# Expert product of a decoder step: every second chunk in plain fp32, and another order of stores, word gathers and row gathers

## What is computed

```python
qry = (hc @ w_query).reshape(-1, PEER_HEADS, 2, PEER_HALF)
...
top_s, pos = lax.top_k(cand_s, PEER_TOPK)
idx = jnp.take_along_axis(cand_i, pos, axis=-1)
gate = jax.nn.softmax(top_s, axis=-1).astype(hc.dtype)
act = jax.nn.gelu(jnp.einsum('cd,chkd->chk', hc, expert_u[idx]))
return jnp.einsum('chk,chkd->cd', gate * act, expert_v[idx])
```

## Time and profile before

| | us |
|---|---|
| median of 3 runs | 2215.64 (2212.16 to 2217.15) |
| the profiled execution's own time | 2217.63 |
| its span, first to last instruction | 2215.9 |
| DVE busy / ACT busy / POOL busy | 1620.5 / 1120.8 / 785.4 |
| PE busy | 2166.3 |
| down stage, pass 0 | 1548.6 to 1896.7 |
| down stage, pass 1 | 1896.7 to about 2198 |

### The profile page before, as it was taken

How to read it: one execution, slowest core, us unless ns; L and a number is a source line. 1 busy time by engine, 2 the same in 40 slices (tenths; PEclk the granted TensorE clock), 3 DMA queues, 4 the chain that set the end, 5 groups by cost and what they waited for, 6 DMA issues and landing times.

```text
span 2215.9 us, 53111 instructions
## 1 busy us (share of the span) xinstructions
PE 2166.3 (98%) x16578; PEld 2128.9 (96%) x16578; DVE 1620.5 (73%) x2983; ACT 1120.8 (51%) x2094; POOL 785.4 (35%) x612
## 2 busy tenths in 40 slices
PE   9999999999999999999999999999889999999997
PEld 8999899999999999999999999999789999999997
DVE  8778688886766767888885444466567787788886
ACT  6445366667455445555555444455333444444453
POOL 0321100002011000888888888200577433222231
PEclk9999999999999999999999999999999999999998
DMA  7887656666556556877776878698899999899995
GB/s 245 292 292 248 224 185 199 207 210 209 182 187 204 176 173 182 192 179 190 189 185 179 204 185 188 179 314 260 273 320 307 350 390 379 313 369 371 369 365 191
DMA packets 303834, 546.01 MB, mean 246 GB/s; under 512 B 77072, under 2 KB 116456, under 8 KB 303600
## 3 DMA queue, kind: packets, MB, share of 16 engines
q1 hardware_dynamic: 227024, 427.68, 59.6%
q0 software_dynamic: 60064, 105.07, 16.0%
q10 hardware_dynamic: 16640, 12.06, 1.8%
HBM read 519.39 MB, written 25.28 MB: 246 GB/s over the span
## 4 chain that ended last, share of the span: by engine, by line
PE 65%; POOL 5%; issue 3%; DMA 2%; DVE 2%; ACT 0%; DVEq 0%; SPq 0%; ACTq 0%
PE ps L317 15%; PE ps L320 15%; PE ps L316 15%; PE ps L2207 8%; PE ps L2220 5%; PE ps L2211 5%; POOL gu L1790 3%; DMA gat<-expert_v,gidx 2%; POOL gat L1639 1%; DVE lo L1623 0%; PE ps L2251 0%; DMA raw<-weights 0%; PE ps L1403 0%; DMA gu<-u_spill,gidx 0%; DVE gacc L2085 0%
## 5 line engine op out<-in xcount | busy, mean ns | idle before, releaser
L304 DVE TENSOR_TENSOR lo<-raw,hi 128x512 fp32r<-128x512 f32 x995 | 685.8, 697 | 365.6 <-ACT hi L299 345.0
L299 ACT CAST hi<-raw 128x512 fp32r<-128x512 f32 x995 | 608.1, 620 | 471.9 <-PE ps L320 447.2
L316 PE MATMUL ps<-h_hi,hi 128*128 128x264 f32 (+1 forms) x3200 | 821.8, 286 | 1.0 <-DVE h_lo L957 1.0
L317 PE MATMUL ps<-h_lo,hi 128*128 128x264 f32 (+1 forms) x3200 | 820.1, 286 | 0.0
L316 PEld LDWEIGHTS ps<-h_hi,hi 128*128 128x128 f32 x3200 | 601.8, 188 | 7.9 <-issue 6.3
L317 PEld LDWEIGHTS ps<-h_lo,hi 128*128 128x128 f32 x3200 | 602.0, 188 | 0.3 <-issue 0.2
L1773 POOL DMA_INDIRECT w_spill<-chosen,widx x256 | 432.4, 1689 | 264.5 <-DVE widx L1998 186.8
L320 PE MATMUL ps<-h_hi,lo 128*128 128x264 f32 (+1 forms) x3200 | 523.3, 285 | 2.1 <-DVE lo L304 1.9
L320 PEld LDWEIGHTS ps<-h_hi,lo 128*128 128x128 f32 x3200 | 444.3, 188 | 3.8 <-DVE lo L304 3.6
L2207 PE MATMUL ps<-whl,hi 128*128 128x368 f32 x1544 | 348.7, 348 | 6.4 <-DVE whl L2077 5.2
L1639 POOL DMA_INDIRECT gat<-expert_v,gidx x160 | 178.0, 1112 | 315.4 <-DVE gacc L2085 297.4
(11 more groups left out here) (308 smaller groups left out, 2294.4 us busy)
## 6 DMA issues: line engine op xcount, KB each, us to landing
raw<-u_tiles SPq DMA_DIRECT2D x512, 256.0 KB
raw<-weights SPq DMA_DIRECT2D x480, 256.0 KB
raw_v<-expert_v SPq DMA_DIRECT2D x128, 512.0 KB
raw<-expert_v SPq DMA_DIRECT2D x124, 512.0 KB
w_spill<-zeros ACTq DMA_DIRECT2D x16, 736.0 KB, 5.6
wld<-w_spill SPq DMA_DIRECT2D x32, 368.0 KB, 4.1
u_spill<-ust SPq DMA_DIRECT2D x128, 40.0 KB
qb<-q_spill POOLq DMA_DIRECT2D x8, 512.0 KB, 5.9
```

What stands on the lines that cost most here:

```text
L299: nc.scalar.copy(hi[k % SPLIT][:], raw_quarter(k)).then_inc(hi_done, 1)
L304: nc.vector.tensor_tensor(lo[k % SPLIT][:], raw_quarter(k), hi[k % SPLIT][:].bitcast(F32), ALU.subtract).then_inc(lo_done, 1)
L316: pe.matmul(out, a, rhs[0][:, first + j, 0:n], start=start and j == 0, stop=False)
L317: pe.matmul(out, a, rhs[1][:, first + j, 0:n], start=False, stop=False)
```

## The change

Plain chunks are 1, 3, 5 and 7 of each turn (not chunk 1 of pass 0 and not the last): 126 of 256. SP stores the last tile of `u_spill` after one load of the stage instead of four. POOL starts rows after 5 words instead of 10; then it issues two words behind each of the first five rows, and from there one and two by turns. There are four row buffers instead of three (the fourth takes the place of a gate buffer that is no longer used). In pass 0 rows are added from step 3 of turn 1 on, four in that turn, five a turn in turns 2 to 7, six in turns 8 to 13. DVE stops for words before turns 1, 2, 4, 7 and 10 (before: 1, 3, 6 and 9). The residual comes back in four loads of 540,672 bytes, all before the loads of turn 4, instead of 16 loads of one sixteenth spread over the pass. The rest of the diff gives all engines one common semaphore for increments that nothing waits for.

```diff
-NATIVE = (3, 7)
+NATIVE = (1, 3, 5, 7)
...
+    gat3 = place("gat3", at["raw_v"] + 2 * 4 * 4 * TD, [P, HALF * P])
+    gacc = place("gacc", at["gat3"], [P, len(GROUPS), HALF * P])
...
-    gat.append(gat2)
+    gat += [gat2, gat3]
+    ROWS = len(gat)
...
-    BOUNDS = (1, 3, 6, 9)
+    BOUNDS = (1, 2, 4, 7, 10)
     FIVE, SIX = (1, 2, 3, 5, 6), (1, 2, 3, 5, 6, 7)
-    ADDS = [[()] + 7 * [FIVE] + 4 * [SIX] + [SIX, FIVE, FIVE, (0, 1, 2, 3, 4)], 15 * [FIVE] + [(0, 1, 2, 3, 4)]]
+    ADDS = [[(), (3, 5, 6, 7)] + 6 * [FIVE] + 6 * [SIX] + [FIVE, (0, 1, 2, 3, 4)], 15 * [FIVE] + [(0, 1, 2, 3, 4)]]
+    WORDS_AT = (0, 5, 15, 30, 50, TG)
...
-        for s in range(RAW, SLOTS):
+        load_expert(0, 0, RAW)
+        spill(PAIR_U - 1, 1)
+        for s in range(RAW + 1, SLOTS):
             load_expert(0, 0, s)
-        spill(PAIR_U - 1, 1)
...
-        sp.dma_start(x2[:, 0], x2_dram[:, 0]).then_inc(x2_in, 16)
-        sp.dma_start(x2[:, KD - 1], x2_dram[:, KD - 1]).then_inc(x2_in, 16)
...
+        x2_back(0)
+        with sp.Fori(1, CHUNKS - UP_CHUNKS - 1) as i:
+            for s in range(SLOTS):
+                load_expert(0, i + 1, s)
+                if s == 2:
+                    sp.wait_ge(w_mul, UP_CHUNKS + i + 4)
+                    cells_in(UP_CHUNKS + i + 1, 1)
+            x2_back(i)
+        x2_back(3)
...
-        for n in range(FIRST_WORDS):
+        words = WORDS_AT[1]
+        for n in range(words):
             gather_u(n)
...
+        for n in range(2 * TG):
+            if n == ROWS - 1:
+                pool.wait_ge(w_mul, UP_CHUNKS + 3)
+            if n >= ROWS:
+                pool.wait_ge(gat_used, n - ROWS + 2)
             gather_rows(n)
-            if n == TG + 2:
+            for _ in range(min(1 if n > ROWS and n % 2 else 2, TG - words)):
+                gather_u(words)
+                words += 1
+            if n == TG + ROWS - 1:
```

More of the change, by code:

```diff
@@ L1489, in mid_vector @@
                 dve.wait_ge(raw2_hi, t + 1)
-                dve.sem_inc(dve_go, 1)
+                dve.sem_inc(go, 1)
                 nc.vector.scalar_tensor_tensor(out=raw2[1][:, t, :], in0=x[:, t, 0:LIVE],
@@ L1548, in program @@
     sel_seen = sem("sel_seen")
-    gat_in, gat_used = [sem(f"gat_in{b}") for b in range(3)], sem("gat_used")
-    gu_in = [sem(f"gu_in{b}") for b in range(4)]
+    gat_in, gat_used = [sem(f"gat_in{b}") for b in range(4)], sem("gat_used")
+    gu_in = [sem(f"gu_in{b}") for b in range(5)]
     gw_made, gacc_zero = sem("gw_made"), sem("gacc_zero")
@@ L1578, in program @@
     G_FIRST = [sum(GROUPS[:g]) for g in range(len(GROUPS))]
-    WORD_TURNS = [-(-sum(len(a) for a in ADDS[0][:i]) // TURN) * TURN for i in BOUNDS] + [TG]
-    FIRST_WORDS = WORD_TURNS[1]
+    assert all(sum(len(a) for a in ADDS[0][:i]) <= n for i, n in zip(BOUNDS[1:], WORDS_AT[1:]))
     def column(n):
@@ L1735, in load_expert, with x2_back @@
             sp.dma_start(expert_slot(s).rearrange("p a b -> p (a b)"), expert_v[p, 8 * i + s]).then_inc(expert_in(s), 16)
-        for s in range(RAW, SLOTS):
+        def x2_back(q):
+            at_q = slice(4 * q, 4 * q + 4) if isinstance(q, int) else bass.ds(4 * q, 4)
+            sp.dma_start(x2[:, at_q], x2_dram[:, at_q]).then_inc(x2_in, 16)
+        load_expert(0, 0, RAW)
+        spill(PAIR_U - 1, 1)
+        for s in range(RAW + 1, SLOTS):
             load_expert(0, 0, s)
-        spill(PAIR_U - 1, 1)
         load_expert(0, 1, 0)
@@ L1744, in experts_sync @@
             load_expert(0, 1, s)
-        sp.dma_start(x2[:, 0], x2_dram[:, 0]).then_inc(x2_in, 16)
-        sp.dma_start(x2[:, KD - 1], x2_dram[:, KD - 1]).then_inc(x2_in, 16)
[L1747 to L1754, removed]
+        x2_back(0)
[7 more added lines that the diff above has]
+        x2_back(3)
+        with sp.Fori(CHUNKS - UP_CHUNKS - 1, NK // 8 - 1) as i:
+            for s in range(SLOTS):
+                load_expert(0, i + 1, s)
         with sp.Fori(0, NK // 8) as i:
@@ L1788, in gather_u @@
         def gather_u(n):
-            j, batch = column(n), max(b for b in range(4) if n >= WORD_TURNS[b])
+            j, batch = column(n), max(b for b in range(len(BOUNDS)) if n >= WORDS_AT[b])
             nc.gpsimd.indirect_dma_start(gu[:, j:j + 1], None, u_rows,
@@ L1792, in gather_u @@
                 .then_inc(gu_in[batch], 16)
-        for n in range(FIRST_WORDS):
+        words = WORDS_AT[1]
+        for n in range(words):
             gather_u(n)
[L1795 to L1798, removed]
-            gather_rows(n)
[L1800 to L1806, removed]
-            if n == TG + 2:
+        for n in range(2 * TG):
[3 more added lines that the diff above has]
+                pool.wait_ge(gat_used, n - ROWS + 2)
+            gather_rows(n)
+            for _ in range(min(1 if n > ROWS and n % 2 else 2, TG - words)):
+                gather_u(words)
+                words += 1
+            if n == TG + ROWS - 1:
                 pool.wait_ge(mm_done, 2 * C0 + 2 * NK + SPLIT)
@@ L2080, in add_rows @@
         def add_rows(n):
-            j, b = column(n), n % 3
+            j, b = column(n), n % ROWS
             g = 0 if j < GROUPS[0] else 1
-            dve.wait_ge(gat_in[b], 16 * (n // 3) + 16)
+            dve.wait_ge(gat_in[b], 16 * (n // ROWS) + 16)
             dve.wait_ge(gat_used, n + 1)
@@ L2088, in weigh_rows @@
         def weigh_rows(b):
-            first, last = WORD_TURNS[b] // TURN, WORD_TURNS[b + 1] // TURN
-            dve.wait_ge(gu_in[b], 16 * (WORD_TURNS[b + 1] - WORD_TURNS[b]))
+            first, last = WORDS_AT[b] // TURN, WORDS_AT[b + 1] // TURN
+            dve.wait_ge(gu_in[b], 16 * (WORDS_AT[b + 1] - WORDS_AT[b]))
             for rows_of in (slice(first, last), slice(GROUPS[0] + (TURN - 1) * first, GROUPS[0] + (TURN - 1) * last)):
@@ L2124, in after_pass @@
             if p == 0:
-                dve.wait_ge(x2_in, 16 * KD)
+                dve.wait_ge(x2_in, 16 * KD // 4)
             def hi_part(m):
```

17 lines of the change are left out of this document (8 added, 9 removed).

## The result

The changed kernel takes 2196.7 us (median of 4, 2194.77 to 2200.54); the kernel before, with one more run beside it, 2214.0 (2212.16 to 2217.15). The ratio is 0.9923, with a 95% interval of 0.9903 to 0.9942: 17 us faster, 0.8%. The forecast was 2195, in a range of 2184 to 2210. The profiled execution took 2195.4 us, span 2193.7.

The account below looks back on a forecast made before the run. POOL's gathers were taken to bound pass 0, with PE waiting through DVE, and PE to bound pass 1. Pass 0 -30 and pass 1 +8.6 gave net -21.5 on 2217.63, 2196; forecast median 2195, range 2184 to 2210 us.

Parts of the forecast that it names:

- The total: Whole kernel: net -21.5 us on the profiled 2217.63 gives 2196; 2195 us forecast for the median.
- Plain chunks on PE: PE, both passes: four chunks take 9.50 us instead of 9.23, 0.27 us for each chunk replaced.
- the count of passes: Skill's four array passes for true fp32: plain product a third dearer, 63 chunks about 47 us, no gain.
- Pass 1, +8.6 us: Pass 1, where PE is the path: 32 split chunks made plain lengthen it by 8.6 us, to about 310.
- PE's sum: PE's work in a pass before the change: 32 groups of four chunks, 295.4 us, and the fold, 3.6: 299.0 us.
- The store and the five words: Start of pass 0: POOL starts about 1553.5, 9.5 us earlier; DVE's 11.8 us stop and PE's 9.64 idle go.
- The stop before turn 10: Pass 0, DVE waiting for all 80 words: DVE stops about 5 us, PE about 2; 4 us for all stops.
- The DMA sum, 318 us: Pass 0's next limit: 285.4 us of bytes at 384 GB/s, 19 for words, 5.6 early idle, 8.3 at the end.
- The residual, 0 (at the other end 4 us): Pass 0, turns 1 to 3: 1.5 MB moved early costs nothing if later turns take it back, else 4 us.
- PE alone: Rival, chance 0.12: the DMAs keep up, pass 0 is 311 us or less, the time 2188 or below.
- New waits on top: Rival, chance 0.11: word stops, early residual and clock falls add; pass 0 328 to 335 us, time 2204 to 2211.
- No change: Rival, chance 0.08: DMAs hold only 332 to 341 GB/s; pass 0 335 to 344 us, time 2211 to 2220.

Follow-up runs that it names:

- half_orders: words_in_time with two plain chunks a turn (3 and 7) and pass 0's loads of expert_v cut to half a chunk from turn 1 on; 2174.0 us.
- plain_first_late: words_in_time with two plain chunks a turn in pass 1 (four in pass 0) and the residual in 16 loads over the pass; 2178.6 us.
- words_in_time: Changed kernel with the last batch of words cut in two: 65 due before turn 10, all 80 before turn 13; 2188.9 us.
- late_store: Changed kernel with the last store of the up products behind four loads again; 2198.5 us, ratio 0.9931 to the kernel before.
- half_loads: words_in_time with each load of expert_v in pass 0 from turn 1 on bringing only half the chunk; 2182.8 us.

## Why the prediction held, and where it did not

- *The total:* 2195 for 2196.7 is better than its parts, and that is luck. Pass 0 fell by 25.9 us instead of 30, pass 1 rose by 3.2 instead of 8.6, and the two errors cancel. (2196 less 2.0 for the median is 2194, not 2195; that changes nothing.)
- *Plain chunks on PE:* right. Four chunks take 9.50 us, pass 1 is 307.2 in six of the eight kernels with four plain chunks a turn in that pass, and the trace decided rightly against the count of passes.
- *Pass 1, +8.6 us:* too much for the two profiled executions, where it was +3.2. The sum took 301.3 us for pass 1 from a window that ended before the last products. To the start of the last sums it was 304.0, of which 5 us were above PE's sum, lost at the fold at the pass's end: DVE's last add came 0.52 us late, and the granted clock from 2194 to 2198 was 0.50. The changed kernel's execution does not lose them, but others do (last section), so part of the +3.2 is chance too. Between executions in which the clock stays up, pass 1 is 299.5 us with two plain chunks (half_orders, plain_first_late) and 307.2 with four: 7.7 us, not far from the 8.6 that the text charged.
- *The store and the five words:* right in every event (1553.13 for 1553.5, no stop before turn 1). But what they are worth was read from the idle PE that they take away, 9.64 us; the store, undone alone, costs 1.7 us of pass 0.
- *The stop before turn 10:* the step that failed. The text had DVE stop 5 us and PE 2, put 4 us down for all stops "and none on top of what follows". DVE stopped 8.16 us, PE idled 6.60, and with the half clock it made most of 8.8 us of pass 0 (322.2 against 313.4). The reckoning let row 48 wait for the add of row 44, some 4 us ahead of the stop. But that add ended at 1743.98, and row 48 only went out at 1746.41: POOL never waited for an add from 1712 to 1758, it was itself behind, and the last word went out 1.1 us after DVE was at the stop.

```profile
1742.70 1.28 DVE L2091 SCALAR_TENSOR_TENSOR gacc<-gat,gw,gacc 128x1024 f32<-128x1024 f32 x1
```

  The same text had worked out that POOL falls behind in turns 8 and 9 (2.7 us a turn at 1.44 us a gather; from 1711.96 to 1747.66 it was 35.70 / 26 = 1.37 us, 20.6 for the 15 gathers of a turn against 19.0 of PE), but did not carry it into the reckoning of the stop.
- *The DMA sum, 318 us:* too long, by 4.6 to 6.6 us. The pass ran in 313.4 us once the stop was gone, and in 311.4 in the best kernel. That 322.2 came near 318 is luck: one term was 5 us or more too long, the other up to 8.8 us too short. A likely reason is in the trace of the changed kernel. The sum took 384 GB/s at share 1.00 as the most and added the words to it, but here more was moved, words among it:

```profile
1610.00:1630.00 20.00, 18.73 (x127) 18.45 (x125) 10.81 (x15) 5.44 (x12) 14.10 (x14) 1.00 1.04 395
```

  That the DMAs are the next limit was right in kind: share 1.00 in words_in_time, 4 to 6 us of it on PE with four plain chunks, 8.6 us with two.
- *The residual, 0 (at the other end 4 us):* some 3 us, nearer the end that was not taken.
- *The rivals:* "PE alone" came nearer to the mechanism than the DMA sum did, but with the new wait on top, so its time, 2188, was only nearly reached when the stop was taken away (2188.9). "New waits on top" named what came, a stop for words, but at 328 to 335 us for pass 0 and not at 322. "No change" did not hold: the pass moved 361 GB/s and not 332 to 341. "DMA: Bandwidth & Descriptors" of the Trainium skill, section Specifications, gives about 358 GB/s as the limit of HBM for one core. The measurements decide against it for this one core: 371 and 374 GB/s over whole passes (words_in_time and plain_first_late).

## What to carry to other kernels

When a producer's queue is relieved, look for the last thing that stands behind the heaviest turns, and ask whether the producer gets there in time by its own pace, not only by what it waits for; a stop may be put later for nothing, as the 80 words show. Do not price a removed wait at its idle time where the DMAs are near full: in late_store the stop lets loads catch up, so part of the gain of taking it away comes back as late loads. Try the parts alone: here the plain chunks gained nothing beside the new orders in one pass and cost 4.5 us in the other, 7.7 where the clock stayed up. And before a few us of one profiled execution are given to a change, look whether the granted clock fell in one execution and not in the other.

## What was not expected of the hardware

The DMAs kept 371 to 374 GB/s up over 311 to 313 us, with gathers and words among the loads: 374 in plain_first_late. The window of its pass 0:

```profile
1548.40:1859.84 311.44, 307.81 (x2081) 306.98 (x2081) 205.36 (x293) 96.71 (x198) 177.27 (x165) 1.00 0.99 374
```

And PE's clock fell at the end of both passes of the kernel before, although it was hardly idle. Windows of the kernel before, the second pass's fold and what follows:

```profile
2186.00:2190.00 4.00, 3.48 (x28) 3.31 (x26) 4.00 (x7) 2.88 (x6) 0.00 (x0) 1.00 0.02 5
2190.00:2194.00 4.00, 4.00 (x28) 4.00 (x27) 1.14 (x2) 1.08 (x2) 0.00 (x0) 0.69 0.02 6
2194.00:2198.00 4.00, 4.00 (x17) 4.00 (x17) 0.00 (x0) 0.00 (x0) 0.00 (x0) 0.50 0.00 0
```

PE was busy from 2190 to 2198, first with the fold's products of 16 and 64 columns, after a wait of 0.52 us, and ran at 0.50 behind them. In the changed kernel the fold follows PE's products without a wait, and pass 1 stays at 1.00. But the wait alone does not decide it. In pass 1 of half_loads the fold comes without a wait, and the four products behind it take 1.57 us at half clock; in half_orders it comes after a wait, and they take 0.91. Half_loads first, then half_orders:

```profile
2159.02 4.07 PE L2260 MATMUL ps<-same,gacc 128*128 128x16 f32 x32
2162.85 1.57 PE L2216 MATMUL ps<-whl,hi 128*128 128x368 f32 x4
```

```profile
2149.39 3.79 PE L2260 MATMUL ps<-same,gacc 128*128 128x16 f32 x32 [0.28 <-DVE gacc L2094]
2152.98 0.91 PE L2216 MATMUL ps<-whl,hi 128*128 128x368 f32 x4
```

Over the 14 profiled executions, with two folds each, the granted clock falls to 0.50 behind the fold in 9 of 28: in 5 of the 22 that come without a wait and in 4 of the 6 that come after one. So the same products bring the clock down in one execution and not in another, and what decides it stays open. Where it came, pass 1 was 1.6 to 4.5 us longer than in executions without it.
